# Two thirds of V's projection moved from one head pair to the next in a fused decoder layer on one NeuronCore

## The reference, cut to what matters

```python
z = h @ lp['w_in']
q = z[..., OFF_Q:OFF_K].reshape(B, T, ATT_HEADS, HEAD_DIM)      # 8 heads x 64
k = z[..., OFF_K:OFF_V].reshape(B, T, ATT_HEADS, HEAD_DIM)
v = z[..., OFF_V:OFF_F].reshape(B, T, ATT_HEADS, HEAD_DIM)
...
s = einsum('bqhd,bkhd->bhqk', q, k) * HEAD_DIM ** -0.5 + dq - dk   # forget bias
p = softmax(where(k_pos <= q_pos, s, -inf))
att = einsum('bhqk,bkhd->bqhd', p, v)
```

## Time and profile before

| | |
|---|---|
| median of 3 runs | 2142.99 us (2140.17 to 2146.22) |
| the profiled execution | 2143.55 us, of which the profile's span is 2141.5 us |
| PE busy | 2027.0 us, 95% of the span |
| DVE, ACT, POOL busy | 792.8, 390.2, 634.9 us |
| share of the chain that ended last | PE 84%, DVE 5%, SP's queue 4%, issue 2%, ACT 2% |
| head pairs | from about 109 us to 408 us |

### The profile page before, as it was taken

How to read it: one execution, slowest core, us unless ns; L and a number is a source line. 1 busy time by engine, 2 the same in 40 slices (tenths; PEclk the granted TensorE clock), 3 DMA queues, 4 the chain that set the end, 5 groups by cost and what they waited for, 6 DMA issues and landing times.

```text
span 2141.5 us, 33016 instructions
## 1 busy us (share of the span) xinstructions
PE 2027.0 (95%) x13046; PEld 1928.5 (90%) x13046; DVE 792.8 (37%) x1424; ACT 390.2 (18%) x699; POOL 634.9 (30%) x490
## 2 busy tenths in 40 slices
PE   5989998799999999999999999999999999999996
PEld 4978887545899999999999998999999999999996
DVE  3445556534100223012621666143324332432236
ACT  3434444322100000000210244000000000000003
POOL 4322020033422232233232533422223232323223
PEclk9999999899999999999999999999999999999997
DMA  9322112287422112241111501111111111111102
GB/s 329 98 68 61 51 31 71 97 271 252 139 79 85 44 40 89 69 128 40 47 50 40 162 1 30 50 50 39 49 39 48 40 43 46 40 48 39 49 30 84
DMA packets 174824, 164.17 MB, mean 77 GB/s; under 512 B 14238, under 2 KB 138610, under 8 KB 174603
## 3 DMA queue, kind: packets, MB, share of 16 engines
q1 hardware_dynamic: 153307, 132.50, 20.1%
q0 software_dynamic: 6400, 17.05, 2.5%
q10 hardware_dynamic: 15032, 13.43, 2.1%
HBM read 149.03 MB, written 14.03 MB: 76 GB/s over the span
## 4 chain that ended last, share of the span: by engine, by line
PE 84%; DVE 5%; SPq 4%; issue 2%; ACT 2%; DMA 1%; POOL 1%; POOLq 0%; ACTq 0%; DVEq 0%
PE psA L1745 11%; PE psA L1749 11%; PE psA L1751 11%; PE psB L1751 10%; PE psB L1749 10%; PE psB L1745 10%; PE psB L1859 2%; PE psB L1862 1%; PE psB L1863 1%; PE psA L1913 1%; PE psB L2023 1%; DVE prob L1267 1%; PE psA L1998 1%; PE ps L1927 1%; SPq L397 1%
## 5 line engine op out<-in xcount | busy, mean ns | idle before, releaser
L627 POOL CAST whi<-raw 128x1024 fp32r<-128x1024 f32 x131 | 136.6, 1043 | 1141.7 <-PE psA L1745 548.9
L628 POOL TENSOR_TENSOR wlo<-raw,whi 128x1024 fp32r<-128x1024 f32 x131 | 320.7, 2448 | 10.5
L1745 PE MATMUL psA<-hhi,whi 128*128 128x364 f32 x1008 | 223.2, 330 | 3.0 <-DVE stat L1351 1.6
L1749 PE MATMUL psA<-hlo,whi 128*128 128x364 f32 x1008 | 223.4, 330 | 0.0
L1751 PE MATMUL psA<-hhi,wlo 128*128 128x364 f32 x1008 | 223.1, 330 | 0.0
L1751 PE MATMUL psB<-hhi,wlo 128*128 128x364 f32 x960 | 213.0, 330 | 0.0
L1749 PE MATMUL psB<-hlo,whi 128*128 128x364 f32 x960 | 212.9, 330 | 0.0
L1745 PE MATMUL psB<-hhi,whi 128*128 128x364 f32 x960 | 212.3, 330 | 0.6 <-DVE alo L1376 0.6
L1630 DVE TENSOR_TENSOR ft<-psB,sil 128x1092 f32<-128x1092 f32 x22 | 28.5, 1296 | 405.9 <-PE psB L1751 399.5
L1745 PEld LDWEIGHTS psA<-hhi,whi 128*128 128x128 f32 x1008 | 174.6, 188 | 3.8 <-issue 3.4
L1751 PEld LDWEIGHTS psA<-hhi,wlo 128*128 128x128 f32 x1008 | 175.8, 189 | 0.0
(11 more groups left out here) (417 smaller groups left out, 3636.6 us busy)
## 6 DMA issues: line engine op xcount, KB each, us to landing
raw<-in_w_in SPq DMA_DIRECT2D x53, 512.0 KB, 3.9
raw<-in_w_gate_up SPq DMA_DIRECT2D x44, 512.0 KB, 3.8
kpage<-in_cache_k SPq DMA_DIRECT2D x64, 256.0 KB, 4.2
vpage<-in_cache_v POOLq DMA_DIRECT2D x64, 256.0 KB, 4.0
ada_late<-in_ada_w SPq DMA_DIRECT2D x8, 2048.0 KB, 8.1
raw<-in_w_down SPq DMA_DIRECT2D x22, 512.0 KB, 3.8
ada<-in_ada_w SPq DMA_DIRECT2D x4, 2048.0 KB, 17.9
x_keep<-xt SPq DMA_DIRECT2D x1, 4368.0 KB, 21.4
```

Of the source, the lines that this page charges most:

```text
L627: link(nc.gpsimd.tensor_copy(whi[slot][:, 0:n, :], raw[slot][:, 0:n, :]))
L628: nc.gpsimd.tensor_tensor(wlo[slot][:, 0:n, :], raw[slot][:, 0:n, :], whi[slot][:, 0:n, :].bitcast(F32), ALU.subtract).then_inc(s["w_split ...
L1745: m = mm(ps[:, c, 0:CH], whi[slot][:, b, :], hi[:, k, c * CH:(c + 1) * CH], start=first, stop=False)
L1749: mm(ps[:, c, 0:CH], whi[slot][:, b, :], lo[:, k, c * CH:(c + 1) * CH], start=False, stop=False)
```

## The change

Before, the 24 slots of pair p hold the work of pair p + 1 in the order Q (slots 0 to 5), K (6 to 11), K's tokens (12 to 14), V (15 to 20), V's tokens (21 to 23). Pair 3's slots are empty, and the head holds all of Q, K and V of pair 0.

After, V's second and third chunk stay with their own pair:

| slots of pair p | before | after |
|---|---|---|
| 0 to 3 | Q of p + 1, chunks 0 and 1 | V of p, chunks 1 and 2 |
| 4, 5 | Q of p + 1, chunk 2 | V's tokens of p, 4 transposes, then 3; V stored |
| 6 to 11 | K of p + 1 | Q of p + 1 |
| 12 to 14 | K's tokens, stored | K of p + 1, chunks 0 and 1 (first half) |
| 15 to 17 | V of p + 1 | K of p + 1, the rest; K split by DVE at 17 |
| 18 to 20 | V of p + 1 | K's tokens of p + 1, stored at 20 |
| 21 to 23 | V's tokens, stored at 23 | V of p + 1, chunk 0, and its first 2 transposes |

Pair 3 has slots 0 to 5 filled, the head makes V's chunk 0 only. V's tokens come in groups of 2, 4 and 2 blocks (with the sample tokens in the last) instead of 4, 4 and the sample. POOL's `values(p, n)` splits them in three steps, of which PE waits for each before the first block that reads it (i = 0, 2 and 6). `scores(0, 0)` waits for 4 token copies instead of 6. The diff, cut to its core:

```diff
+VTOK = (slice(0, 2), slice(2, 6), slice(6, QT))
+VEARLY = 6
...
-            def values(p):
+            def values(p, n):
-                pool.wait_ge(s["tok_copied"], 6 * p + 6)
-                if p:
-                    pool.wait_ge(s["o_done"], p * QT)
+                at = VTOK[n]
+                pool.wait_ge(s["tok_copied"], 6 * p + 4 + n)
+                if n == 0:
+                    if p:
+                        pool.wait_ge(s["o_done"], p * QT)
...
+            def value_tokens(p, n):
+                bank, at = qkv_bank(p, (10, 13, 14)[n]), VTOK[n]
+                act.wait_ge(s["tok_tr"], 6 * p + 4 + n)
+                to = tok[:, at, :].rearrange("p a b -> p (a b)")
+                if n < 2:
+                    nc.scalar.copy(to, bank[:, 0:P * (at.stop - at.start)]).then_inc(s["tok_copied"], 1)
+                    return
+                link(nc.scalar.copy(tok[0:NS, QT, :], bank[0:NS, 2 * P:3 * P]))
+                nc.scalar.copy(to, bank[:, 0:2 * P]).then_inc(s["tok_copied"], 1)
+                act.wait_ge(s["tok_copied"], 6 * p + 6)
+                stores(p, "v_prompt", "v_sample", s["vst"])
...
             def qkv(p):     # ACT
...
+                yield
+                act.wait_ge(s["kl_done"], p + 1)
+                act.wait_ge(s["tok_tr"], 6 * p + 3)
+                kv_copy(p, 9, 0, "v_done")
+                yield
+                act.wait_ge(s["kst"], 32 * (p + 1))
+                value_tokens(p, 0)
+                yield
+            def later_values(p):
+                for c in (1, 2):
                     yield
+                    kv_copy(p, 10 + c, c, "v_done")
                     yield
+                for n in (1, 2):
+                    value_tokens(p, n)
                     yield
...
-                fill = qkv(p + 1) if p + 1 < HP else iter(())
+                fill = chain(later_values(p), qkv(p + 1) if p + 1 < HP else ())        # ACT and PE
+                fill = chain([None] * VEARLY, qkv(p + 1) if p + 1 < HP else ())        # DVE
...
+            def later_values(p):     # PE
+                for c in (1, 2):
+                    yield from gemm_chunk(p, 10 + c, (U_QKV + 3 * p + 2) % RING, c, "v_done")
+                token_major(p, 13, 6, range(2, 6))
+                yield
+                token_major(p, 14, 6, range(6, 8), 2 * P)
+                yield
...
-                        pe.wait_ge(s["tok_copied"], 6)
+                        pe.wait_ge(s["tok_copied"], 4)
...
-                if i == 0:
-                    pe.wait_ge(s["vl_done"], p + 1)
+                for n, at in enumerate(VTOK):
+                    if i == at.start:
+                        pe.wait_ge(s["vl_done"], 3 * p + n + 1)
```

More of the change, by code:

```diff
@@ L16 @@
 from contextlib import ExitStack
+from itertools import chain
 import numpy as np
@@ L676, in _ @@
                     one(u_)
-                values(p)
+                for n in range(3):
+                    values(p, n)
                 if p + 1 < HP:
@@ L821, in token_major @@
                     return
-                nc.scalar.copy(tok[0:NS, QT, :], qkv_bank(p, use)[0:NS, 0:P]).then_inc(s["tok_copied"], 1)
-                act.wait_ge(s["tok_copied"], 6 * p + 3 * which + 3)
+                nc.scalar.copy(tok[0:NS, QT, :], bank[0:NS, 0:P]).then_inc(s["tok_copied"], 1)
+                act.wait_ge(s["tok_copied"], 6 * p + 3)
+                stores(p, "k_prompt", "k_sample", s["kst"])
+            def value_tokens(p, n):
[9 more added lines that the diff above has]
+                stores(p, "v_prompt", "v_sample", s["vst"])
@@ L1865, in gemm_chunk, with token_major @@
                 yield
[L1867 to L1871, removed]
+            def token_major(p, use, ready, blocks, sample_at=None):
+                pe.wait_ge(*qkv_previous(p, use))
+                pe.wait_ge(s["kv_done"], 6 * p + ready)
                 bank = qkv_bank(p, use)
-                if g < 2:
-                    for j in range(4):
-                        n = 4 * g + j
-                        m = tr(bank[:, j * P:(j + 1) * P], kv[:, n * P:(n + 1) * P], ident[:, :])
-                else:
-                    m = tr(bank[0:NS, 0:P], kv[:, NP:TU], ident[:, :])
+                for j, n in enumerate(blocks):
+                    m = tr(bank[:, j * P:(j + 1) * P], kv[:, n * P:(n + 1) * P], ident[:, :])
+                if sample_at is not None:
+                    m = tr(bank[0:NS, sample_at:sample_at + P], kv[:, NP:TU], ident[:, :])
                 m.then_inc(s["tok_tr"], 1)
@@ L1883, in qkv @@
                 u0 = U_QKV + 3 * p
-                for j, done in enumerate(("q_done", "k_done", "v_done")):
+                for j, done in enumerate(("q_done", "k_done")):
                     if not (p or j):
@@ L1888, in qkv @@
                     for c in range(3):
[L1889 to L1893 removed]
+                        yield from gemm_chunk(p, 3 * j + c, (u0 + j) % RING, c, done)
+                for g, blocks in enumerate((range(4), range(4, 8), ())):
+                    token_major(p, 6 + g, 3, blocks, 0 if g == 2 else None)
+                    yield
+                unit(u0 + 2)
+                yield from gemm_chunk(p, 9, (u0 + 2) % RING, 0, "v_done")
+                token_major(p, 10, 4, range(2))
+                yield
[3 more added lines that the diff above has]
+                token_major(p, 13, 6, range(2, 6))
+                yield
+                token_major(p, 14, 6, range(6, 8), 2 * P)
+                yield
             def scores(p, i):
@@ L1959, in _ @@
             for p in range(HP):
-                fill = qkv(p + 1) if p + 1 < HP else iter(())
+                fill = chain(later_values(p), qkv(p + 1) if p + 1 < HP else ())
                 for n in range(NTILE):
```

64 lines of the change are left out of this document (29 added, 35 removed).

## The result

The changed kernel takes 2147.55 us (median of 20 runs, 2141.41 to 2151.78). The kernel before, on the same chips, takes 2138.95 us (20 runs, 2135.97 to 2146.22). The ratio is 1.0038, with a 95% interval of 1.0030 to 1.0047: slower, by about 8.1 us. (The ratio is not simply that of the two medians, which differ by 8.6 us.) That lies just outside the 0.3% that the prediction took for "same", and the interval begins at it.

A forecast was written before the change was run, and what follows sets the result against it. It took PE, with its idle and low-clock time from the head to pair 3's end, as the bound. The terms -8.4 + 4.5 - 0.5 + 5.7 = +1.3 us on 2143.55 gave 2144.8, by median 2144.5; range 2137 to 2152.

The forecast's parts named there:

- Step 1: Head: work leaves it, so PE's first transposes come 8.4 us earlier, at 105.0 us, capped by DVE's scan.
- Step 2: Pairs 0 to 2: PE's waits grow from 6.2 to 7.7 us, losing 1.5 us a pair, 4.5 in all.
- slot 4's 0.4: Slot 4 of each pair: turning V waits 0.4 us for ACT's copy of the chunk ended in slot 3.
- block 2's 1.1 and 0.5: Scores of block 2: too little filling, 1.1 us wait for normalise, then 0.5 until ACT empties Q's bank.
- Q's 1.2: Q's chunks: PE's waits for their evacuation fall from 1.6 to 1.2 us a pair.
- block 6's 2.0 and 1.1: Block 6: K's split on DVE delays pt_low; block 4's waits move here at the same size, 2.0 and 1.1 us.
- Block 7's: Block 7: ACT's copy, K's stores and decay loads delay o_copy(6) and pt_hi(14); 1.4 us of wait left.
- rival B: Low clock behind block 6's transposes and waits, about 2 us a pair: +7.3 us, 2151; chance 0.16.
- Step 3: Into pair 3: the 0.46 us wait for a late decay row goes, gaining 0.5 us.
- Step 4: Pair 3: moved V work mostly shows, since about 9 us of work hide 3.5; loses 5.7 us.
- A: Rival: head's gain kept, pair 3 loses only 3 to 4 us, pairs 0 to 2 nothing: 2137.5; chance 0.14.
- C: Rival: POOL 2 us late for values(0, 0), or table load not hidden; head gains 6.2: +3.5, 2147; chance 0.16.

The follow-up runs named there:

- best2: best1 with the sample group's scan on DVE moved behind the first two normalise of pair 0; ratio to the kernel before 0.9997.
- decay_first: Changed kernel with the two decay loads issued on ACT ahead of slot 20's piece instead of behind it; ratio to the kernel before 1.0010.
- heat7: Changed kernel plus twelve matmuls nobody reads ahead of tile 15's transposes in pairs 0 to 2; ratio to the kernel before 1.0027.
- all_late: Changed kernel with decay loads first, K's stores in slot 21 and V's stores behind pt_hi(5); ratio to the kernel before 1.0009.
- k_late: Changed kernel with K's two stores issued in slot 21, behind pt_hi(14), instead of slot 20; ratio to the kernel before 1.0021.
- thin3: Changed kernel with pair 3's second and third chunk of V made with 12 instead of 48 matmuls; ratio to the kernel before 1.0022.
- best1: Changed kernel with decay loads ahead of slot 20's piece, V's stores behind pt_hi(5), K split on DVE by chunks; 2133.09 us, ratio to before 0.9980.
- before_split3: Kernel before the change with only K's split on DVE done chunk by chunk; ratio to the kernel before 0.9986.
- split_only: Changed kernel with decay loads first and K split by chunks, V's stores left in slot 5; ratio to the kernel before 0.9993.
- best1_again: best1 unchanged, run once more on the chip of split_only; 2133.47 us, ratio to the kernel before 0.9968.

## Why the prediction was off where it was

**Step 1, the head: right.** 8.9 us against 8.4 (over all profiles the first transposes came at 102.58 to 105.24 us with the new head and at 111.78 and 113.37 with the old one, so a single pair of executions can be a microsecond or two off), with the same bound in the same place: DVE's scan, and `scores_max` directly behind it. 0.4 us of it is that the scan itself started earlier, 100.67 against 101.05. best2 corrects one thing: the scan isn't the only cap. The decay row lands at nearly the same time, so without the scan nothing more is to be had.

**Step 2, pairs 0 to 2: the step that failed, in a clock that it put at nothing and in the size of one wait.** I had the pairs at 79 to 81 us; they took 83.86, 81.70 and 82.22. I had 7.7 us of waits a pair; pair 1 has 8.06. Term by term, predicted and measured: slot 4's 0.4 and 0.42; block 2's 1.1 and 0.5 and 1.07 and 0.16; Q's 1.2 and 1.15; block 6's 2.0 and 1.1 and 2.00 and 1.07. These could be read off the trace of before, by what each moved piece hid and stood behind. Block 7's was 1.4 and came as 2.19, because I priced the issue of K's stores (1.11 us) from a row and let the decay loads behind them cost what they had cost elsewhere, beside an exponential. In the new order they had no such cover, and took 1.6 to 2.2 us. The row at 94.66 us of the trace of before (1.66 us behind two stores) had that price. decay_first shows the cause: undoing that order alone gives back 2.8 in 1000 of the 3.8.

The longer wait by itself is small: over three pairs the waits came to 1.4 us more than forecast, the lower clock to 5.2, of which heat7 places 4.2 behind block 7's wait. That larger part is what I had as **rival B**: a low clock, about 2 us a pair, 2151. By its size, and in part by the prediction's own sign for it (the clock falls in blocks 6 and 7), B is what happened; it had a chance of 0.16. Its price was nearly right (1.3 to 1.6 us) and its place mostly wrong. In the profiled execution of after the clock falls behind block 7's wait, not in block 6; in all_late, heat7 and k_late it falls in block 6, in three pairs, one and one. The Trainium skill (TensorE: Matmul & The Clock Gate, "HAM oscillation — how this bites in real kernels") warns that waits in TensorE's work drop the clock and make the next block of matmuls start cold. Behind block 7 the trace agrees: the gap of 2.19 us in pair 0 stands ahead of a clock of 0.59, though the waits in the page's example are longer. Behind block 6 it mostly doesn't: after 2.00 us in pair 0 the scores of block 7 took 2.02 us, as at full clock. I had set that warning aside because one stretch of before, with a wait of 2.07 us, had kept its clock. That row was a fact about one place in one execution; it didn't say that another gap, at another place, would be free as well. heat7 shows the link from wait to clock: with the wait filled, the clock stayed up in block 7 of all three pairs, and nothing else had been changed.

So my sum was +1.3 (added to the median of 2142.99 it gives 2144.3, not the 2144.5 written there); with the measured 10.6 in place of 4.0 it is +6.7 (the head and pair 3 come to 0.5 and 0.8 less than I had). The ratio says +8.1 us, within what the wandering clock does to one profiled execution.

**Step 3, into pair 3: right.** No wait for a decay row ahead of pair 3. It lies inside the length of pair 2 and is not measured apart from it.

**Step 4, pair 3: right.** 4.9 us against 5.7. From first transposes to the scores of block 2 went 363.35 - 352.24 = 11.11 us; I had computed 11.25. Behind that pair 3 is 0.4 us shorter than before, where I had 0.2 longer: V's stores cost more (2.58 us of wait) and the clock gave more back (0.92 instead of 0.82). That these two cancelled is luck; in the other profiles with V whole and V's stores in slot 5 pair 3 took 61.28 to 69.14 us. thin3 confirms that most of the moved matmuls are on the path there.

**Rivals A and C.** C's first half was absent: PE waits 0.16 us for POOL in `values(0, 0)`, and in best1 0.54. They meet at 113.6 us, as counted (114), and best2 shows what it costs when POOL is late. A needed pairs that lose nothing and is refuted as the change stands; but best1, with the same placement of V and a better order on ACT and DVE, is 4.3 to 6.8 us faster than before.

**Is the placement itself a gain?** Not settled. before_split3 has the cheap part of best1 in the old order and reaches 0.9986; best1, on the same chip, has 0.9980, and 0.9968 on another. The difference is 1.3 us by these ratios and 2.3 by the medians on the same chip, and 3.8 us in the second case. The intervals overlap in both, so the 2 us by which best1 was to be faster are not shown. Open as well is what decides whether the clock falls in block 6, block 7 or not at all: it differs between executions of kernels that are alike there.

## What to carry to other kernels

Price a DMA issue by where it will stand in its engine's queue, not by what it costs where it stands now: two loads that cost nothing beside an exponential held ScalarE for 1.6 us behind two stores, and the engine that the kernel is bound by paid for it twice, in the wait and in its clock. Look in the whole trace for a place where the same instructions already stand in the new order; here the head had one. When work is moved out of one stretch, list what the compute engine will meet in the new one, and price the low clock behind each new gap, with a chance of its own, even where one gap of that size was seen to be harmless. Here the head gave 8.9 us and the tail took back 4.9; the 10.6 us in between decided. Look too whether the order on the side engines, changed alone, gives as much.

## What the runs showed of the hardware

- The issue of two decay loads on ACT took 0.81 to 0.91 us where they stood ahead of K's stores (pairs 0 to 2 of decay_first), and 1.61, 1.62 and 2.17 us behind them (after). In the heads of the eleven profiles in which they stand behind the stores they took 1.62 to 1.70 us; in the heads of k_late and all_late, ahead of the stores and with no exponential beside them, 0.35 + 0.46. So it is the place behind the stores that goes with the longer time, not the missing exponential. With the stores alone in front of it, `o_copy` waited 1.11 us in pairs 0 and 1; with both, 2.77.
- The second of two stores took 0.61 us in most places. In pair 3, V's took 1.80 us (after) and 2.01 (split_only) in slot 5, but 0.61 in decay_first and k_late; behind `pt_hi(5)` it took 1.97 us in best1 and 0.61 in best1_again, which are the same kernel. In pair 2, K's took up to 1.58 us (decay_first) while SP was issuing loads. What makes it long stays open.
- A wait of 2.0 us in block 6 with transposes around it is followed by a clock of 0.57 over 4 us in one execution (heat7, pair 1), and in others the scores of block 7 behind it took 2.02 to 2.03 us, as at full clock (after, decay_first). It was low in five of eighteen pairs. A mean of many runs is needed to price it; a single profile isn't enough.
